# Holding one expert's weights for two passes at a fixed place, and bias products of 32 rows

## The reference

```python
# D_MODEL = D_FF = 1024, N_EXPERTS = 32, TOP_K = 4, 256 tokens, all float32
logits = h @ w_r + b_r
top_v, top_i = lax.top_k(logits, TOP_K)
comb = one_hot(top_i) weighted by softmax(top_v)          # (256, 32)
for e in range(N_EXPERTS):
    z = h @ w1[e] + b1[e]                                 # w1[e]: 1024 x 2048
    glu = jnp.minimum(z[:, :D_FF], 7.0)
    lin = jnp.clip(z[:, D_FF:], -7.0, 7.0)
    act = glu * jax.nn.sigmoid(1.702 * glu) * (lin + 1)
    out = out + comb[:, e:e + 1] * (act @ w2[e] + b2[e])  # w2[e]: 1024 x 1024
```

## Time and profile before

| | us |
|---|---|
| median of 3 runs | 1369.27 (1367.04 to 1369.98) |
| profiled execution, its own time | 1369.35 |
| its span, first to last instruction | 1367.3 |
| PE busy / DVE busy / ACT busy in the span | 1289.8 / 347.7 / 216.0 |
| DMA in the stretch 457 to 1340 us | 421 GB/s |

### The profile page before, as it was taken

The page is one execution under the profiler, slowest core; times in us unless marked ns, Lnnn a source line. Parts: engine busy times, 40 slices in busy tenths (PEclk is TensorE's granted clock), DMA queues, the critical chain, the costliest instruction groups (busy, mean ns, idle before and its releaser), DMA issues.

```text
span 1367.3 us, 13118 instructions
## 1 busy us (share of the span) xinstructions
PE 1289.8 (94%) x5600; PEld 554.4 (41%) x5600; DVE 347.7 (25%) x605; ACT 216.0 (16%) x357; POOL 27.9 (2%) x74
## 2 busy tenths in 40 slices
PE   5999999999889999999999999999999999999995
PEld 2445588777433333333333333233333323333331
DVE  2657687221421211121112111112111111211112
ACT  2157631110210100010000100001100000110001
POOL 2000001000000000000000000000000000000000
PEclk9999999999969999999999999999999999999999
DMA  9632569687259999999999999999999999999994
GB/s 350 234 101 90 193 223 388 244 330 306 92 213 394 421 421 422 421 422 421 421 421 421 421 421 421 421 422 420 421 422 421 420 422 421 420 422 421 422 420 187
DMA packets 100009, 488.56 MB, mean 357 GB/s; under 512 B 9104, under 2 KB 43088, under 8 KB 46192
## 3 DMA queue, kind: packets, MB, share of 16 engines
q1 hardware_dynamic: 95568, 468.40, 84.4%
q0 software_dynamic: 2848, 18.88, 3.6%
q10 hardware_dynamic: 1536, 0.46, 0.2%
HBM read 486.65 MB, written 1.05 MB: 357 GB/s over the span
## 4 chain that ended last, share of the span: by engine, by line
PE 52%; DMA 38%; ACT 4%; DVE 4%; SPq 1%; issue 1%; DVEq 0%; ACTq 0%
DMA arena<-in_exp_w 34%; PE bank L665 18%; PE bank L580 9%; PE bank L677 8%; DMA arena<-in_w_in 3%; PE bank L647 2%; PE bank L711 2%; PE bank L569 2%; PE bank L511 2%; PE bank L688 2%; SPq L355 1%; PE bank L542 1%; PE bank L723 1%; PE bank L655 1%; ACT arena L829 1%
## 5 line engine op out<-in xcount | busy, mean ns | idle before, releaser
L665 PE MATMUL bank<-arena,temps 128*64 128x512 f32 x2112 | 471.8, 596 | 26.0 <-DMA arena<-in_exp_w 25.8
L665 PEld LDWEIGHTS bank<-arena,temps 128*64 128x64 f32 x2112 | 147.1, 137 | 345.7 <-issue 264.7
L677 PE MATMUL bank<-arena,temps 128*64 128x512 f32 x1056 | 233.9, 595 | 0.7 <-DVE temps L1292 0.6
L1285 DVE TENSOR_SCALAR temps<-bank 128x512 f32<-128x512 f32 x33 | 22.8, 692 | 743.9 <-PE bank L665 743.9
L677 PEld LDWEIGHTS bank<-arena,temps 128*64 128x64 f32 x1056 | 72.8, 137 | 138.4 <-issue 132.0
L580 PE MATMUL bank<-arena 128*128 128x256 f32 x512 | 113.1, 383 | 3.3 <-DMA arena<-in_w_in 3.3
L917 ACT ACTIVATE temps<-temps 128x512 f32<-128x512 f32 x33 | 20.8, 629 | 554.4 <-DVE temps L1285 554.4
L580 PEld LDWEIGHTS bank<-arena 128*128 128x128 f32 x512 | 98.3, 192 | 19.1 <-issue 5.6
L647 PE MATMUL bank<-vtokb,hot 128*64 128x512 f32 x264 | 66.9, 629 | 0.0
L688 PE MATMUL bank<-temps,hot 64*128 64x512 f32 x264 | 65.6, 615 | 0.8 <-ACT temps L923 0.8
L711 PE MATMUL bank<-b1r,bsel 128*64 128x512 f32 x264 | 64.0, 607 | 0.5 <-issue 0.5
(11 more groups left out here) (229 smaller groups left out, 801.9 us busy)
## 6 DMA issues: line engine op xcount, KB each, us to landing
arena<-in_exp_w SPq DMA_DIRECT2D x396, 1024.0 KB, 26.5
arena<-in_w_in SPq DMA_DIRECT2D x20, 1024.0 KB, 6.4
arena<-in_w_mod POOLq DMA_DIRECT2D x16, 1024.0 KB, 7.8
arena<-in_w_mod SPq DMA_DIRECT2D x8, 1024.0 KB, 16.1
arena<-in_w_pool_proj SPq DMA_DIRECT2D x4, 1024.0 KB, 5.0
arena<-in_w_rnn_proj SPq DMA_DIRECT2D x4, 1024.0 KB, 6.5
arena<-in_w_out SPq DMA_DIRECT2D x4, 1024.0 KB, 10.0
arena<-in_lru_wa SPq DMA_DIRECT2D x8, 256.0 KB, 3.3
```

The source lines that it names most:

```text
L665: last = mm(psum[4 + q][h * SLOTS:(h + 1) * SLOTS, :], xg[:, k // 4, k % 4, :], wslot[s][:, q, h * HALF:(h + 1) * HALF], start=False, stop ...
L677: last = mm(psum[6][h * SLOTS:(h + 1) * SLOTS, :], actT[:, k // 4, k % 4, :], wslot[s][:, kk, h * HALF:(h + 1) * HALF], start=(k == 0), st ...
L1285: v.tensor_scalar(glu, psum[4][:, :], LIMIT, None, ALU.min).then_inc(glu_ready, 1)
```

## The change

One expert with more than 64 tokens and a number of at least 2 (`pick`; expert 2 if there is none) changes places with expert 2, and its two passes are items 2 and 3. Both use the same 12 chunks, which are loaded once: a place is a set of 12 loads, and items 2 and 3 share place 2. `place_of` and `place_done` turn items into places and a place into the last item that uses it. There are 33 fixed items (`NP`) and 32 places. Experts beyond place 1 are read from `tabE` by SP, POOL and DVE. The further entry of `pick` is taken out of the list, so `more` is 0 and again 33 items run: 0 to 30 as straight code, 31 in the loop, 32 last. Beside this, each product of the first bias takes only the 32 rows of its quarter.

```diff
+TWICE = 2
+NP = E + 1
+FIXED = NP - 2
+LAST = (E - 2) * CPI
...
+        def place_of(i):
+
+            return i if i <= TWICE else i - 1
+
+        def place_done(q):
+
+            return q if q < TWICE else q + 1
+
+        def load_no(i, c):
+
+            return (place_of(i) if isinstance(i, int) else E - 2) * CPI + c
...
-            for n in range(WSLOTS, E * CPI):
-                sp.wait_ge(w_used, n - WSLOTS + 1)
-                load_expert(n // CPI, n // CPI, n % CPI)
-            sp.wait_ge(items_ready, 1)
-            last_item = sp.value_load(more[0:1, 0:1], min_val=0, max_val=MORE - 1) + (E - 1)
-            with sp.Fori(E, last_item + 1) as i:
+            for q in range(1, E - 1):
+                if q == TWICE:
+                    sp.wait_ge(items_ready, 1)
+                e = q if q < TWICE else sp.value_load(tabE[0:1, q + (q > TWICE):q + (q > TWICE) + 1], min_val=0, max_val=E - 1)
+                for c in range(CPI):
+                    n = q * CPI + c - WSLOTS
+                    if n >= 0:
+                        sp.wait_ge(w_used, place_done(n // CPI) * CPI + n % CPI + 1)
+                        load_expert(q, e, c)
+            last_item = sp.value_load(more[0:1, 0:1], min_val=0, max_val=MORE - 1) + (NP - 1)
+            with sp.Fori(NP - 1, last_item + 1) as i:
                 e = sp.value_load(tabE[0:1, ds(i, 1)], min_val=0, max_val=E - 1)
                 for c in range(CPI):
                     sp.wait_ge(w_used, (i - 1) * CPI + (c + 1))
-                    load_expert(i, e, c)
+                    load_expert(E - 2, e, c)
...
                 for q in range(4):
                     h = q % 2
-                    mm(psum[4 + q // 2][h * SLOTS:(h + 1) * SLOTS, :], bselq[:, q, :], b1r[:, :], start=True, stop=False)
+                    r = slice(q * E, (q + 1) * E)
+                    mm(psum[4 + q // 2][h * SLOTS:(h + 1) * SLOTS, :], bselq[r, q, :], b1r[r, :], start=True, stop=False)
...
+            num = ecol[0:MORE, 0:E]
+            link(v.tensor_tensor(turn, ovr[:, 0, :], num, ALU.mult))
+            link(v.tensor_reduce(pick, turn, AX.X, ALU.max))
+            link(v.tensor_scalar(pick, pick, float(TWICE), None, ALU.max))
+            v.tensor_scalar(away, pick, -float(TWICE), None, ALU.add)
+            v.tensor_scalar(back, pick, -1.0, float(TWICE), ALU.mult, ALU.add)
+            link(v.scalar_tensor_tensor(ovr[:, 0, :], num, pick, ovr[:, 0, :], ALU.not_equal, ALU.mult))
+            v.tensor_scalar(turn, num, pick, back, ALU.is_equal, ALU.mult)
+            v.tensor_scalar(same, num, pick, None, ALU.is_equal)
+            link(v.tensor_scalar(place, num, float(TWICE), away, ALU.is_equal, ALU.mult))
+            link(v.tensor_tensor(place, place, turn, ALU.add))
+            link(v.tensor_tensor(place, place, num, ALU.add))
...
+            link(v.tensor_tensor(exc, exc, same, ALU.subtract))
...
                     if isinstance(i, int):
-                        e1, r1 = i + 1, 0
+                        e1, r1 = i + 1, int(i == TWICE)
+                        if i + 1 >= TWICE:
+                            e1 = dve.value_load(tabE[0:1, i + 1:i + 2], min_val=0, max_val=E - 1)
```

More of the change, by code:

```diff
@@ L31 @@
 MORE = 16
-ITEMS = E + MORE
+CPI = 12
+TWICE = 2
+NP = E + 1
+FIXED = NP - 2
+LAST = (E - 2) * CPI
+ITEMS = NP + MORE
 EPS = 1e-6
@@ L38 @@
 BANK = 512
-CPI = 12
 HALF = 512
-LAST = (E - 1) * CPI
 NSLOT = 18
@@ L198, in build @@
         tabf = RB[0:MORE, 384:386]
+        turn = RB[0:MORE, 448:480]
+        place = RB[0:MORE, 480:512]
+        same = RB[0:MORE, 544:576]
+        pick, away, back = (RB[0:MORE, 512 + n:513 + n] for n in range(3))
         ixu = sb("ixu", [P, 16], U32)
@@ L314, in build @@
         assert [key for key, c in chunk_no.items() if c >= NF - RING] == [("rp", c) for c in range(4)]
+        def place_of(i):
[4 more added lines that the diff above has]
+            return (place_of(i) if isinstance(i, int) else E - 2) * CPI + c
         def slot_of(i, c):
-            return ((i if isinstance(i, int) else E - 1) * CPI + c) % WSLOTS
+            return load_no(i, c) % WSLOTS
         def landed_at(i, c):
             if isinstance(i, int):
-                return 16 * ((i * CPI + c) // WSLOTS + 1)
-            return i * 16 + 16 * ((LAST + c) // WSLOTS + 1 - (E - 1))
+                return 16 * (load_no(i, c) // WSLOTS + 1)
+            return i * 16 + 16 * ((LAST + c) // WSLOTS + 1 - FIXED)
         def expert_src(e, c):
@@ L352, in _, with load_expert @@
         def _(sp):
-            def load_expert(i, e, c):
-                s = slot_of(i, c)
+            def load_expert(q, e, c):
+                s = (q * CPI + c) % WSLOTS
                 sp.dma_start(wslot[s], expert_src(e, c)).then_inc(expert_landed[s], 16)
@@ L475, in _ @@
             bias_rows_of(0)
-            for i in range(E - 1):
+            for i in range(FIXED):
                 pool.wait_ge(w_used, i * CPI + 1)
[L478 to L481, removed]
+                if i + 1 < TWICE:
+                    bias_rows_of(i + 1)
+                else:
+                    if i + 1 == TWICE:
+                        pool.wait_ge(items_ready, 1)
+                    bias_rows_of(pool.value_load(tabE[0:1, i + 1:i + 2], min_val=0, max_val=E - 1))
+            last_item = pool.value_load(more[0:1, 0:1], min_val=0, max_val=MORE - 1) + (NP - 1)
+            with pool.Fori(FIXED, last_item) as i:
                 pool.wait_ge(w_used, i * CPI + 1)
@@ L745, in _ @@
             item(0, first=True)
-            for i in range(1, E - 1):
+            for i in range(1, FIXED):
                 item(i)
-            last_item = pe.value_load(more[0:1, 0:1], min_val=0, max_val=MORE - 1) + (E - 1)
-            with pe.Fori(E - 1, last_item) as i:
+            last_item = pe.value_load(more[0:1, 0:1], min_val=0, max_val=MORE - 1) + (NP - 1)
+            with pe.Fori(FIXED, last_item) as i:
                 item(i)
@@ L925, in _ @@
             take_tokens(0)
-            for i in range(E - 1):
+            for i in range(FIXED):
                 item(i)
             act.wait_ge(items_ready, 1)
-            last_item = act.value_load(more[0:1, 0:1], min_val=0, max_val=MORE - 1) + (E - 1)
-            with act.Fori(E - 1, last_item) as i:
+            last_item = act.value_load(more[0:1, 0:1], min_val=0, max_val=MORE - 1) + (NP - 1)
+            with act.Fori(FIXED, last_item) as i:
                 item(i)
@@ L1258, in _ @@
             v.tensor_copy(combT, b[0:E, 0:SEQ]).then_inc(read_dve, 1)
-            v.tensor_copy(tabE[:, 0:E], ecol[0:1, 0:E])
-            v.memset(tabR[:, 0:E], 0)
+            v.tensor_copy(tabE[:, 0:TWICE + 1], place[0:1, 0:TWICE + 1])
+            v.tensor_copy(tabE[:, TWICE + 1:NP], place[0:1, TWICE:E])
+            v.memset(tabR[:, 0:NP], 0)
             dve.wait_ge(table_done, 1)
-            v.tensor_copy(tabE[:, E:ITEMS], psum[7][0:1, 0:MORE])
-            v.tensor_copy(tabR[:, E:ITEMS], psum[7][0:1, MORE:2 * MORE]).then_inc(items_ready, 1)
+            v.tensor_copy(tabE[:, NP:ITEMS], psum[7][0:1, 0:MORE])
+            v.tensor_copy(tabR[:, NP:ITEMS], psum[7][0:1, MORE:2 * MORE]).then_inc(items_ready, 1)
             dve.wait_ge(items_ready, 1)
@@ L1295, in item @@
                     weighted(e1, r1)
-            for i in range(E - 1):
+            for i in range(FIXED):
                 item(i)
-            last_item = dve.value_load(more[0:1, 0:1], min_val=0, max_val=MORE - 1) + (E - 1)
-            with dve.Fori(E - 1, last_item) as i:
+            last_item = dve.value_load(more[0:1, 0:1], min_val=0, max_val=MORE - 1) + (NP - 1)
+            with dve.Fori(FIXED, last_item) as i:
                 item(i)
```

## The result

The changed kernel takes 1359.16 us (median of 5 runs, 1357.71 to 1361.23) against 1369.27 (5 runs, 1365.23 to 1370.44). The ratio is 0.9933, with a 95% interval of 0.9918 to 0.9949: 0.67% faster, where 1360.1 us had been forecast. The profiled execution took 1357.71 us.

A forecast was written before the change was run, and what follows sets the result against it. Loads were taken to bound the kernel: 30.0 us saved by 12 fewer loads, 20.7 given back as DMA's rest, so 1369.35 - 9.2 = 1360.1 us. Own range 1357.3 to 1362; 8 in 10, 1357 to 1365.5.

The forecast's parts named there:

- The loads as the bound: From the 43rd load on, the experts' weight loads set the pace at 2.502 us each; PE's time counts only until then.
- The 12 loads and the rest: Dropping 12 loads saves 30.0 us; DMA idling on a full ring until the 43rd load gives back 20.7.
- the sum: 43rd load lands at 488.1, then 341 loads at 2.502 us; last lands at 1341.3, 9.2 us earlier; end at 1360.1.
- item 0: First item, its bias at half clock until near 398 us: 0.8 us saved.
- the 18.85 us behind the last load: Time from the last load's landing to the end, in which nothing is changed: 18.85 us.
- The bias: First bias products of each item: 0.86 us plus 0.35 for shape switches, 1.21 in all, 0.51 less an item.
- The four-tile row: Existing products with four column tiles, eight records in 1.97 us at half clock; taken as showing that four tiles halve the time.
- The rival that quarters of one bank exclude each other: Only bias quarters of different banks overlap: bias 2.50 us, end 5.3 us later than forecast, 1365.4 us; chance 0.08.
- The front: Before item 0, twelve small DVE instructions add 2.1 us, hidden behind PE's own turns with 1.1 us cover left: nothing.
- The reads of `tabE`: Reads on SP, DVE and POOL in the experts' part, hidden by loads in flight or ahead of their users: nothing.
- When PE begins to wait: PE busy without a gap until about 870 us, then waits at each item's chunks 5 to 7.

The follow-up runs named there:

- hold: The kernel before, all 396 loads, with only the 43rd load made to wait for chunk 0 of item 3 instead of item 2: 1391.52 us, ratio 1.0180.
- place 15: The changed kernel with the shared place at 15 instead of 2 (items 15 and 16): 1336.11 us, ratio 0.9777.
- place 26: The changed kernel with the shared place at 26 instead of 2: 1349.98 us, ratio 0.9852.
- place 15 with the 128-row bias: The changed kernel with the shared place at 15 and the 128-row bias products of before: 1339.57 us, ratio 0.9779.
- the place alone: The changed kernel with the 128-row bias products of before, shared place still at 2: 1361.12 us, ratio 0.9952.

## Why the prediction was right

**The loads as the bound, 2.502 us a load.** Held: 2.502 in the changed kernel too, behind the rest.

**The 12 loads and the rest.** Forecast: the 43rd load lands 20.7 us late, the end comes 9.2 us early. Trace: 485.9 - 467.4 = 18.5 us late and 1350.5 - 1339.2 = 11.3 early. The median moved by 10.1 us. The hold experiment measured the rest by itself, place 15 the saving without it. The mechanism held; that the forecast came within 1 us of the median is closer than these runs can tell (the interval is 1358.0 to 1362.3) and in part luck, since two terms of 2 to 3 us that the sum did not have are found below.

**Where the trace beat the sum by 2.1 us.** The slot came free 2.9 us sooner than forecast (480.5 against 483.4), and the load then took 5.4 us to land, not 4.7. The rest itself was not shorter: 21.7 us against 20.7 forecast. The whole chain stood 3 us earlier, the 42nd load too (461.7 against 464.9). As far as the traces tell, the 2.9 us are not the change's: the step of the sum that was mis-sized is item 0, 0.8 us forecast where the first load came 3.9 us earlier. In the profiled execution of before, the granted clock was at 0.50 from 390 to 398 us; in the changed kernel's it was 0.99, so item 0's bias ran at full clock and the first used chunk let SP issue at 395.2 instead of 399.1. The new code of the front does not decide it. The hold experiment, whose code is that of before up to there, has 1.00, and two versions with the new front, place 26 and place 15 with the 128-row bias, have 0.50 in the same stretch:

```profile
390.00:398.00 8.00, 7.44 (x40) 3.30 (x42) 0.66 (x4) 1.88 (x2) 0.40 (x1) 1.00 0.23 74
...
390.00:398.00 8.00, 6.67 (x24) 2.68 (x24) 2.13 (x12) 2.48 (x3) 0.00 (x0) 0.50 0.01 2
```

(The first row is hold, the second place 15 with the 128-row bias.) So the level at which item 0 starts differs from run to run and moves the whole chain behind it by some 3 us, which can be a good part of the 3 to 5 us by which the runs of one kernel differ. What decides the level is not shown. The forecast of the median was nearer (1360.1 against 1359.16) than that of the trace.

The end has a second such term. The prediction took the 18.85 us behind the last load as fixed. They were 18.5 in the changed kernel's trace, but 20.6 in hold's, where the granted clock was 0.72 in the mean of the 6 us in which the last loads landed:

```profile
1367.00:1373.00 6.00, 5.43 (x20) 2.15 (x22) 0.69 (x1) 0.38 (x1) 0.00 (x0) 0.72 0.24 102
```

In the changed kernel's it stayed at 1.00 there. The traces of the place alone and of place 15 also show 0.72 there and 20.1 us.

**The bias, 1.21 us forecast.** Measured 1.02, with the second switch, 0.15, inside `first_map`: 1.17 in all, 0.55 saved an item instead of 0.51. The four-tile row from the kernel's other end was the right neighbour, L698 the wrong one. The rival that quarters of one bank exclude each other is refuted: two groups of four records need quarters 0 and 1 in bank 4 at the same time from two row groups. The Trainium skill, TensorEngine Tiling (Array Packing), Gotcha 1: PSUM Pressure, says that different row tiles cannot access the same PSUM bank simultaneously; for tiles that write different partitions of a bank the measurement, 1.02 us against the 2.50 of that rival, decides against it. Two row groups writing the same partitions of a bank were not tried.

**The front.** The twelve instructions pushed the end of DVE's list to 390.98 us:

```profile
390.64 0.34 DVE L1298 TENSOR_REDUCE RB<-RB 16x2 f32<-16x192 f32 x1
```

2.1 us were forecast, and 390.98 - 388.81 = 2.17 came. L771 (the old L742) starts at 391.43, right behind PE's turns as before, though these ran at full clock here and ended 0.5 us sooner; the cover of 1.1 us had shrunk to 0.45 and was still enough.

**The reads of `tabE`** cost nothing that shows: DMA moves 421 GB/s in the changed kernel (outside its rest) and at place 15 as before.

**When PE begins to wait.** About 870 us was forecast; of PE's 31.7 us of waits on loads 2.6 lie between 470 and 860 already and 29.1 behind it.

## What to carry to other kernels

A transfer saved is worth its time only if the queue can go on with the next one: keeping data for a second use closes its buffers for as long, so ask what the ring holds at that moment and how long it can run from what is free. Where the consumer works off a lead first and is fed just in time later, put such a reuse where the lead is small or gone but enough work remains behind it to use the new lead: here one number, 2, 8, 15 or 26, gave 1359, 1341, 1336 and 1350 us (0.993, 0.980, 0.978 and 0.985 of before; 8 and 15 can't be told apart by time). And a single moved wait, which no engine notices when it happens, can be costed by running it alone.

## What the runs showed of the hardware

- Four 32-row, 64-column tiles in four row groups, two column groups and two banks ran at once: eight float32 records of 512 columns in 1.02 us, against 1.72 with 128-row tiles. Two row groups wrote one bank at the same time, each its own partitions.
- A load issued into resting DMA landed after 4.7 to 5.4 us; late in the kernel, with many loads in flight, one landed after about 26, and the loads followed each other at 2.502 us.
- The same code stood at a granted clock of 0.50 in one execution and of 1.00 in another from 390 to 398 us, just where item 0 begins.
- Behind the last load, in the last item, the granted clock was 0.72 in the mean of 6 us in three of the traces (the place alone, hold, place 15) and 1.00 in others; what remained behind that load was 20.1 to 20.6 us against 18.5 to 18.9.
